# Head norms of a hybrid decoder trunk: the mean squares from one matmul with a constant block matrix, root and reciprocal over all columns

## The reference, cut to what matters

```python
# SSD: one norm over all 256 channels
y = rms_norm(y * jax.nn.silu(z), p['ssd_norm'])
# retention: four heads of 64 channels, centred first
mu = jnp.mean(of, axis=-1, keepdims=True)
var = jnp.mean(jnp.square(of - mu), axis=-1, keepdims=True)
on = ((of - mu) * lax.rsqrt(var + EPS)).reshape(b, l, RET_WIDTH) * p['ret_norm']
# gated linear attention (GLA): four heads of 64 channels
on = of * lax.rsqrt(jnp.mean(of * of, axis=-1, keepdims=True) + EPS)
on = on.reshape(b, l, GLA_WIDTH) * p['gla_norm']
```

## Time and profile before

| what | before |
|---|---|
| median of 3 runs | 1337.65 us (1336.28 to 1340.45) |
| profiled execution, own time | 1338.89 us |
| its span, first to last instruction | 1337.1 us |
| mean granted clock of TensorE | 0.988 |
| TensorE, VectorE, ScalarE, GpSimd busy | 97%, 64%, 53%, 22% of the span |
| slots 35 to 49 in the two layers | about 165 to 244 us, and 821 to 899 us |

### The profile page before, as it was taken

One profiled execution on the slowest core, in us unless ns is written; L12 is line 12 of the kernel. 1 busy time (PEld: TensorE's weight loads), 2 busy tenths in 40 slices (PEclk: granted clock), 3 DMA queues, 4 the chain that ended last, 5 costly groups with the idle time before them and its releaser, 6 DMA issues.

```text
span 1337.1 us, 26923 instructions
## 1 busy us (share of the span) xinstructions
PE 1300.0 (97%) x10781; PEld 1248.4 (93%) x10781; DVE 855.7 (64%) x1696; ACT 706.6 (53%) x1207; POOL 292.5 (22%) x248
## 2 busy tenths in 40 slices
PE   7999999999999999999999999999999999999996
PEld 7988898999999999999998888889999999999996
DVE  6844766478853785388647546755788358835864
ACT  7625464566642674266554264556676247624741
POOL 1100100112242224224411010001123412341250
PEclk9999989999999999999999999999999999999998
DMA  8856645557753775376566566446578347734741
GB/s 270 211 114 145 149 110 122 115 133 158 172 150 83 171 168 158 77 169 171 141 139 146 119 149 165 96 113 143 118 166 187 111 107 166 190 111 103 169 124 67
DMA packets 63387, 189.73 MB, mean 142 GB/s; under 512 B 7584, under 2 KB 8864, under 8 KB 63264
## 3 DMA queue, kind: packets, MB, share of 16 engines
q0 software_dynamic: 27936, 67.12, 30.6%
q1 hardware_dynamic: 30672, 111.95, 26.7%
q10 hardware_dynamic: 4656, 8.95, 2.2%
HBM read 180.33 MB, written 5.43 MB: 139 GB/s over the span
## 4 chain that ended last, share of the span: by engine, by line
PE 76%; DVE 11%; ACT 5%; DVEq 4%; issue 2%; DMA 2%; ACTq 1%
PE bank L1602 41%; PE bank L1631 27%; DMA raw<-weights 1%; DVE ct L955 1%; DVE up L1475 1%; PE bank L1545 1%; ACT wh L537 1%; DVE lru_x L955 1%; ACT wl L536 1%; DVE tz L1471 1%; DVEq L1444 1%; PE bank L1919 1%; DMA wl<-weights 1%; PE bank L1925 0%; DVE wsum L1372 0%
## 5 line engine op out<-in xcount | busy, mean ns | idle before, releaser
L508 POOL DMA_DIRECT2D wl<-weights x194 | 168.4, 868 | 898.5 <-ACT wl L536 897.0
L1602 PE MATMUL bank<-xh,wh 128*128 128x272 f32 x800 | 244.6, 306 | 8.0 <-DVE xl L910 7.6
L537 ACT ACTIVATE wh<-raw 128x512 fp32r<-128x512 f32 (+1 forms) x243 | 198.2, 816 | 92.1 <-PE bank L1602 83.1
L1602 PE MATMUL bank<-xh,wl 128*128 128x272 f32 x800 | 236.2, 295 | 0.0
L1602 PE MATMUL bank<-xl,wh 128*128 128x272 f32 x800 | 235.1, 294 | 0.0
L536 ACT ACTIVATE wl<-raw 128x512 fp32r<-128x512 f32 (+1 forms) x194 | 147.1, 758 | 129.0 <-PE bank L1602 116.9
L1631 PE MATMUL bank<-xh,wh 128*128 128x272 f32 x704 | 203.3, 289 | 1.4 <-ACT p L793 1.4
L1631 PE MATMUL bank<-xh,wl 128*128 128x272 f32 x704 | 203.2, 289 | 0.0
L1631 PE MATMUL bank<-xl,wh 128*128 128x272 f32 x704 | 202.6, 288 | 0.0
L537 ACT ACTIVATE wh<-wsum 128x512 fp32r<-128x512 f32 x176 | 105.3, 623 | 130.1 <-DVE wsum L1372 89.5
L1602 PEld LDWEIGHTS bank<-xh,wh 128*128 128x128 f32 x800 | 155.3, 194 | 19.3 <-issue 17.6
(11 more groups left out here) (401 smaller groups left out, 3011.9 us busy)
## 6 DMA issues: line engine op xcount, KB each, us to landing
raw<-weights SPq DMA_DIRECT2D x202, 512.0 KB, 6.2
wl<-weights POOLq DMA_DIRECT2D x132, 256.0 KB, 5.7
wl<-weights POOLq DMA_DIRECT2D x62, 512.0 KB, 7.3
h<-x SPq DMA_DIRECT2D x4, 544.0 KB, 6.0
y<-h SPq DMA_DIRECT2D x4, 544.0 KB, 2.7
rv<-rk ACTq DMA_DIRECT2D x8, 136.0 KB, 2.7
tz<-rq ACTq DMA_DIRECT2D x8, 136.0 KB, 5.3
S<-s_ssd ACTq DMA_DIRECT2D x2, 512.0 KB, 6.6
```

Of the source, the lines that this page charges most:

```text
L508: nc.gpsimd.dma_start(wl[:, place(j)], weights[n][:, lo:lo + width], accum_op=ALU.add).then_inc(lo_added[BLOCK0[j] % RING], 16)
L537: a(wh[:, place(j)], whole, ACT.Copy).then_inc(hi_done, 1)
L1602: ins = mm(bank_, wt[:, at:at + P], xx[:, cols], start=(i == 0 and pass_ == 0), stop=(i == len(ks) - 1 and pass_ == 2))
```

## The change

The mean over channels is taken by a matmul whose weights are a constant and whose moving operand is the squares, so that it comes out on all 128 partitions at once: head_mean (128x128, 1/64 within each block of 64) for GLA and retention, mean_of_two (all 1/256, the two tiles added up in PSUM) for SSD. ScalarE then takes the root of the whole PSUM tile in place, with epsilon as the bias, VectorE the reciprocal of the whole tile in place followed by a drain, and normed is as before. The stages gla_stat, ssd_stat and ret_stat, head_stat, head_spread and norm_rstd are gone; the slots of the norms stay. SSD's squares now wait until GLA's last mean has been computed, since both use sq, and retention's means wait for the last copy out of M[1].

```diff
-at_slot(35, "gla_stat")
-at_slot(39, "ssd_stat")
-at_slot(47, "ret_stat")
...
-                def norm_root(i, n):
-                    act.wait_ge(n_mean.sem, n_mean.at(layer, i + 1))
-                    a(rstd[:, 0:n], rstd[:, 0:n], ACT.Sqrt).then_inc(n_root.sem, 1)
+                def norm_root(i, *means):
+                    act.wait_ge(n_spread.sem, n_spread.at(layer, i + 1))
+                    for mean in means:
+                        ins = a(mean, mean, ACT.Sqrt, bias=eps[:])
+                    ins.then_inc(n_root.sem, 1)
+                def gla_norm(i):
+                    norm_root(i, M[4][:] if i < 2 else M[4][:, 0:2 * NS])
+                def ret_norm(_=None):
+                    norm_root(5, M[0][:], M[1][:], M[2][:, 0:2 * NS])
...
                 def ssd_squares(_=None):
                     act.wait_ge(n_in.sem, n_in.at(layer, 1))
+                    act.wait_ge(n_spread.sem, n_spread.at(layer, 3))
                     squares(xbc[:, 0:2, :])
                 def ssd_norm(i):
+                    norm_root(3 + i, M[4][:, 0:NS] if i else M[4][:])
...
-                def norm_rstd(i, each, width):
...
+                def inverse(*roots):
+                    for root in roots:
+                        v.reciprocal(root, root)
+                    dve.drain()
...
                 def gla_norm_(i):
-                    dve.wait_ge(n_spread.sem, n_spread.at(layer, i + 1))
+                    dve.wait_ge(n_root.sem, n_root.at(layer, i + 1))
+                    inverse(M[4][:] if i < 2 else M[4][:, 0:2 * NS])
                     if i < 2:
                         ins = normed(gv[:, i, :], prompt, par(layer, "gla_norm", i), M[4][:])
...
                 def ssd_norm_(i):
+                    inverse(M[4][:, 0:NS] if i else M[4][:])
...
                 def ret_norm_(_=None):
-                    dve.wait_ge(n_spread.sem, n_spread.at(layer, 6))
+                    dve.wait_ge(n_root.sem, n_root.at(layer, 6))
+                    inverse(M[0][:], M[1][:], M[2][:, 0:2 * NS])
...
-                def head_stat(i):
-                def head_spread(out, c, t):
-                def ssd_stat(_=None):
...
                 def gla_norm_(i):
...
                     if i < 2:
-                        for c in range(4):
-                            ins = head_spread(M[4][:, c * P:(c + 1) * P], c, i)
+                        ins = mm(M[4][:], cst("head_mean"), sq[:, i, 0:SEQ], start=True, stop=True)
                     else:
                         for t in range(2):
-                            ins = head_spread(M[4][:, t * NS:(t + 1) * NS], SAMPLE, t)
+                            ins = mm(M[4][:, t * NS:(t + 1) * NS], cst("head_mean"), sq[:, t, SEQ:TOK], start=True, stop=True)
...
                 def ssd_norm_(i):
+                    pe.wait_ge(n_used.sem, n_used.at(layer, 3 + i))
+                    cols = slice(SEQ, TOK) if i else slice(0, SEQ)
+                    for t in range(2):
+                        ins = mm(M[4][:, 0:NS] if i else M[4][:], mean_of_two[:], sq[:, t, cols], start=(t == 0), stop=(t == 1))
...
                 def ret_norm_(_=None):
-                    pe.wait_ge(n_rstd.sem, n_rstd.at(layer, 3))
+                    pe.wait_ge(n_sq.sem, n_sq.at(layer, 3))
+                    pe.wait_ge(cent_last.sem, cent_last.at(layer, 1))
                     for t in range(2):
-                        for c in range(4):
-                            head_spread(M[t][:, c * P:(c + 1) * P], c, t)
-                        ins = head_spread(M[2][:, t * NS:(t + 1) * NS], SAMPLE, t)
+                        mm(M[t][:], cst("head_mean"), sq[:, t, 0:SEQ], start=True, stop=True)
+                        ins = mm(M[2][:, t * NS:(t + 1) * NS], cst("head_mean"), sq[:, t, SEQ:TOK], start=True, stop=True)
...
+    put("head_mean", (p // 64 == q // 64) / 64.0)
```

More of the change, by code:

```diff
@@ L265, in trunk @@
         gla_last = sb("gla_last", [2, NSEQ])
-        rstd = sb("rstd", [20])
-        ones = sb("ones", [1])
+        rstd = sb("rstd", [5])
+        ones, eps = sb("ones", [1]), sb("eps", [1])
+        mean_of_two = sb("mean_of_two", [P])
         sq_sum = sb("sq_sum", [TOK])
@@ L405, in trunk @@
         n_in = signal("n_in", 1)
[L406 to L407 removed]
+        n_sq, n_root = signal("n_sq", 3), signal("n_root", 6)
         n_spread = signal("n_spread", 6)
         n_used = signal("n_used", 6)
[L410 to L411 removed]
+        cent_mm, cent_first, cent_second, cent_out, cent_last = (
+            signal(n, 1) for n in ("cent_mm", "cent_first", "cent_second", "cent_out", "cent_last"))
         x_rounded, exact_done = sem("x_rounded"), sem("exact_done")
@@ L904, in _ @@
             v.memset(ones[:], 1.0)
+            v.memset(mean_of_two[:], 1.0 / 256)
+            v.memset(eps[:], EPS)
             dve.drain()
@@ L1297, in ssd_norm_ @@
                 def ssd_norm_(i):
-                    dve.wait_ge(n_spread.sem, n_spread.at(layer, 4 + i))
+                    dve.wait_ge(n_root.sem, n_root.at(layer, 4 + i))
+                    inverse(M[4][:, 0:NS] if i else M[4][:])
                     for t in range(2):
@@ L1909, in ret_b_ @@
                     ins.then_inc(ret_b.sem, 1)
-                def head_stat(i):
[L1913 to L1920, removed]
-                def head_spread(out, c, t):
[L1923 to L1928, removed]
                 def gla_norm_(i):
                     if i == 0:
-                        pe.wait_ge(n_rstd.sem, n_rstd.at(layer, 1))
+                        pe.wait_ge(n_sq.sem, n_sq.at(layer, 1))
                     else:
@@ L1935, in gla_norm_ @@
                     if i < 2:
-                        for c in range(4):
-                            ins = head_spread(M[4][:, c * P:(c + 1) * P], c, i)
+                        ins = mm(M[4][:], cst("head_mean"), sq[:, i, 0:SEQ], start=True, stop=True)
                     else:
                         for t in range(2):
-                            ins = head_spread(M[4][:, t * NS:(t + 1) * NS], SAMPLE, t)
+                            ins = mm(M[4][:, t * NS:(t + 1) * NS], cst("head_mean"), sq[:, t, SEQ:TOK], start=True, stop=True)
                     ins.then_inc(n_spread.sem, 1)
-                def ssd_stat(_=None):
[L1944 to L1950, removed]
                 def ssd_norm_(i):
                     if i == 0:
[L1954 to L1960, removed]
+                        pe.wait_ge(n_sq.sem, n_sq.at(layer, 2))
+                    pe.wait_ge(n_used.sem, n_used.at(layer, 3 + i))
+                    cols = slice(SEQ, TOK) if i else slice(0, SEQ)
+                    for t in range(2):
+                        ins = mm(M[4][:, 0:NS] if i else M[4][:], mean_of_two[:], sq[:, t, cols], start=(t == 0), stop=(t == 1))
                     ins.then_inc(n_spread.sem, 1)
```

25 lines of the change are left out of this document (9 added, 16 removed).

## The result

The changed kernel takes 1376.2 us (median of 4 runs, 1374.31 to 1377.13) against 1338.6 of the kernel before in the same measurement (4 runs): a ratio of 1.028, 95% interval 1.0266 to 1.0295. It is slower by 37.6 us; the forecast was slower, 1370, with a range of 1350 to 1388. The profiled execution took 1377.13 us with a span of 1375.3.

The account below looks back on a forecast made before the run. TensorE, busy for 97%, was taken as the bound, with VectorE's queue deciding; new waits of 24.2 us less 0.9, 5.7 and 3.1, plus 1.6 for a clock fall, gave +16.1 a layer: 1370 us, range 1350 to 1388.

Parts of the forecast that it names:

- late reciprocals: The forecast itself, chance 0.66: long reciprocals in VectorE's queue make TensorE wait, 1370 us.
- TensorE's matmuls: Per layer, three statistics go, 6.3 us, and the wider means add 0.6: net -5.7 us.
- waits, net of before's: TensorE in slots 35 to 49 and OUT0: 24.2 us of new waits a layer, less 0.9 of old ones.
- clock: Falls after GLA's and SSD's statistics go, -3.1 us a layer; one in the output projection costs 1.6.
- Reciprocal: VectorE's reciprocal over 512 columns in the norms, priced at 5.9 ns a column on a fixed 160: 3.2 us.
- Rival B: Each 512-column reciprocal on VectorE takes the upper bound, 4.4 us: 1382 us in all, chance 0.14.
- Rival D: A long reciprocal runs as fast as a multiply, 0.7 us; about 10 us a layer come back: 1350, chance 0.06.
- at ret_aS: Slots 41 to 43: VectorE's queue delays TensorE, ready at 220.55, until 223.6: wait of 3.1 us.
- in OUT0: Output projection: retention's low parts come late after root and reciprocals, so TensorE waits 4.7 and 3.1 us.
- rival C: The clock still falls after the means, or after each wait on the path: 3 us a layer more, 1376, chance 0.07.
- Table loads: ScalarE's 1.28 us load before a root: nothing where ScalarE is idle, in full where it comes late.
- Rival E: VectorE and ScalarE finish before TensorE returns, so TensorE's -8.8 us a layer counts in full: 1321, chance 0.04.

Follow-up runs that it names:

- e2: The changed kernel with each reciprocal replaced by a copy in place, the root kept: 1360.5 us, ratio 1.0152 to the kernel before.
- e1: The changed kernel without root and reciprocal, VectorE multiplying by the bare mean square: 1335.9 us, ratio 0.9967 to the kernel before.
- e3: The changed kernel with root and reciprocal in one ScalarE instruction (Abs_reciprocal_sqrt), VectorE only draining and multiplying: 1346.7 us, ratio 1.0052.
- e6: The change made for GLA alone, SSD and retention as in the kernel before: 1355.3 us, ratio 1.0123.
- e7: The change made for SSD alone, GLA and retention as in the kernel before: 1349.9 us, ratio 1.0083.
- e9: e3 with SSD's norm, retention's norm and the two RG-LRU scans in other slots: 1336.7 us, ratio 0.9988 to the kernel before.
- e8: The change made for retention alone, GLA and SSD as in the kernel before: 1355.7 us, ratio 1.0129.
- e4: The changed kernel with root and reciprocal as exp(-log/2), two ScalarE passes and two table loads: 1369.0 us, ratio 1.022.
- e11: The kernel before, unchanged, run once more for a second profile: 1339.7 us, one run.

## Why the prediction was right, point by point

**Sign, size and place** are right: 1370 forecast, 1376.2 measured. The mechanism is the one forecast, late reciprocals in VectorE's queue; that the total came within 6 us is in part luck, since terms missed in both directions. The slots were to grow by 16.1 a layer and grew by 14.7 and 14.1. In layer 0, term by term:

| term, us in layer 0 | forecast | measured |
|---|---|---|
| TensorE's matmuls | -5.7 | -5.1 |
| waits, net of before's | +23.3 | +17.1 |
| clock | -3.1 + 1.6 | +2.7, the rest of the 14.7 (from the windows, 6.1 less 3.4) |
| sum | +16.1 | +14.7 |

**Reciprocal**: 3.2 forecast from the slope of the earlier trace rows, 3.35 measured. Rival B's 4.4 and the reading of the Trainium skill behind it (VectorE: DVE Perf Modes, First, the fixed hardware budget; an estimate of 8.3 ns a column) come out too high: 6.3 ns a column. The page says that the operation is iterated and gives no time; that it is far slower than a multiply the trace shows, 3354 against some 745 ns for the same columns. Rival D's 0.7 is e2 in effect, with 698 ns: the 10 us a layer that D was to bring back are 9.4 and 8.8. Its time was put at 1350 and is 1360.5, since the slots kept 10.7 and not 12, and 11.2 came elsewhere.

**Waits**: the list, forecast against measured: 0.5 / 0.8 for ScalarE's copy, 0.5 / 0.9 for n_used, 3.7 / 3.5 before ret_b of chunk 1, 3.9 / 2.8 at the GLA sample mean, 3.5 / 1.1 before ret_b of chunk 2, 1.2 / 1.6 at SSD's, 3.1 / 0 at ret_aS, 4.7 + 3.1 / 5.0 + 2.4 in OUT0. The places are right but for ret_aS. **The term that was mis-sized is the clock, and it corrects the waits.** I wrote that falls ahead of another wait "hide in it" and added 1.6 for the one in OUT0. The window 190 to 197 shows what happens instead: TensorE works there at 0.50 until the next wait and behind it, its work takes twice as long, it arrives later, and the waits at GLA's samples and before chunk 2's ret_b come out 1.1 and 2.4 shorter. At ret_aS it is another fall, which I had not forecast, the one after SSD's wait of 1.6: it takes 1.5 us, and TensorE arrives at 223.9, when VectorE is ready. In layer 1 the same wait of 1.6 has no fall behind it (1.00 in the window 887.8 to 893), and ret_aS waits:

```profile
PE bank L1875 <- DVEq L1270: 1.2, 1, 1.2
```

So the clock accounts for some 1.3 of the 3.1 that are missing there. Another 1.3 is that SSD's sample mean, which waits for VectorE, starts at 213.9 and not at my 212.6. Most of the 6.2 less of waits is thus time that went to the clock, which has 4.2 more, and not all. TensorE's busy time says the same without the walk: after and e1 have the same 10539 matmuls, and after's take 10.6 us longer (1301.6 against 1291.0).

**Gone from the clock** are, as forecast, the falls right after slots 35 and 39; the first half of rival C, that the long means would bring them back, is not met (1.00 from 173 to 187). Its second half, a fall after each wait on the path, is near to what happened, but not each wait had one, and the clock took much of its time out of the waits, so the slots came to less than the forecast, not to 3 more. That its value, 1376, is the one measured is in part chance, as the next point but one shows.

**Table loads**: 1.28 us each, ahead of the wait where ScalarE was idle (173.68, its operand came at 175.8), late where ScalarE was late (187.71), as costed. The Trainium skill (ScalarE: Activation LUTs, What ACT_TABLE_LOAD costs) makes its 2.66 of 1.28 for the load and 1.38 for a drain. The trace agrees on the load; the drain is found in none of the norms' rows, where the root starts 1.29 after the load's start (187.71 and 189.00).

**The error of 6 us** is not in the slots, which came out 3.3 us below the forecast in the two layers together, but elsewhere: 9.4 us that no step of mine had. Two layers' output projections (from the first addition to the first SwiGLU product) have 3.4 of them, the SwiGLU parts 3.9, the end 1.6. The 3.4 are the clock once more. The fall that follows OUT0's waits goes on past the first addition: window 264 to 266 above, and in layer 1 at 0.50 from 937 to 941. From the granted clock that costs 1.0 and 2.4 us, and the two parts grew by 1.0 and 2.3. The versions without retention's long waits, e1, e3, e6, e7 and e9, are at most 0.2 longer there; e8, retention alone, has 2.2 and 1.4. So where I had 1.6 us a layer for falls, the clock took 7.1 and 8.1 (6.1 + 1.0 and 5.7 + 2.4).

The SwiGLU parts are less clear. Two profiles of the kernel before differ by up to 1.3 in one part, but e1 to e4 and e9 too have 5 to 11 elsewhere, 5 to 8 of it in the two SwiGLU parts. TensorE's waits for weights, taken over the whole execution, are longer in those kernels; before, after and e9:

```profile
PE bank L1631 <- DMA wl<-weights: 2.0, 3, 1.0
```

```profile
PE bank L1639 <- DMA wl<-weights: 4.0, 5, 1.4
```

```profile
PE bank L1637 <- DMA wl<-weights: 5.5, 7, 1.2
```

That would make 2 to 3.5 us of it, but the second profile of before (e11) has 3.3 there too, so 1.3 of that is within the spread. The rest is open, and so is why the weights would land later where the slots ahead took a different time; no experiment was made on it. It is also where e9's 8.7 us of the slots became 2.0.

**Rival E** was wrong in its price too, and this is the finding that the forecast did not have: with every reciprocal and root gone (e1), not 8.8 but 4.4 us a layer come back, because VectorE's queue between two ret_b stages was the bound of these slots already: 2.3 of the difference are waits, 1.5 the fall behind one of them, 0.6 my reckoning of TensorE's work. The 0.4 us wait of the earlier trace rows was to be read as: there is no slack here, in either direction.

## What to carry to other kernels

A small operation that becomes wide to save a spread must be priced by its own cost per column, taken as a slope from two shapes of the same instruction in the trace; the reciprocal had 6.3 ns a column where the norm's multiply has 1.0 (744 ns for 512, 241 for 32). Before a saving on the busiest engine is counted, look whether another engine's queue sets the end of that stage: a wait of a few tenths of a microsecond in the list can be the only sign, as it was here. Where waits of 3 us follow each other, count the clock between and behind them and not the waits alone.

## What the runs showed of the hardware

The reciprocal's time grows close to linearly from 5 to 512 columns (191 ns, 277 for 19, 367 for 32, 535 for 64, 3354 for 512; those from 32 up in PSUM). A reciprocal square root is one ScalarE instruction at the root's price, 660 ns for 512 columns. And the granted clock stayed at 0.50 to 0.58 for 10 us of slots 38 and 39, from within a wait of 3.5 and over one of 2.8, where every fall of the kernel before in these slots was over after 3.4 us. A fall did not follow every such wait: 1.6 us at SSD's samples had one in layer 0 and none in layer 1, 2.2 us before ret_b in e3 had none, and 2.0 in e1 had one.
